# Cached pages compressed in runs of four and of two instead of one at a time, in a two-layer decoder trunk on one core

## The reference, cut to what matters

```
even layer:  xn = rms_norm(h);  q, k, v, z_a, u_b, v_b, z_b = xn @ w_in_ab     # 2048 x 9216
             dilated attention (A), spatial gating (B);  h += [A, B] @ w_out_ab
             h += sigmoid(h @ w_ple_gate[0]) * (p[0] @ w_ple[0])
odd layer:   the same frame around sparse attention (C), whose compressed branch reads
             pages = cache_c_cmp_kv[page_table]          # 8 rows x 16 pages of 128 x (K, V) x 4 heads x 128
             k_cmp, v_cmp = compress(pages, cw_k), compress(pages, cw_v)
compress:    block i = sum over 32 rows, i*16 .. i*16+31, of row * weight[row of the block, head]
```

## Time and profile before

| | |
|---|---|
| runs | 1836.01 us median, 1835.28 to 1836.19 |
| profiled execution | 1836.29 us, of which the span of instructions is 1834.6 us |
| mean granted clock | 0.989 |
| busy, share of the span | PE 96%, PEld 87%, DVE 59%, ACT 45%, POOL 10% |
| chain that ended last | PE 82%, DVE 12%, ACT 3%, issue 2%, DMA 1% |
| page matmuls (L1738) | 2432, one every 20 to 40 ns when they run |
| projection matmuls (L1712) | 9216 |
| DMA | 406 MB, mean 222 GB/s |

### The profile page before, as it was taken

How to read it: one execution, slowest core, us unless ns; L and a number is a source line. 1 busy time by engine, 2 the same in 40 slices (tenths; PEclk the granted TensorE clock), 3 DMA queues, 4 the chain that set the end, 5 groups by cost and what they waited for, 6 DMA issues and landing times.

```text
span 1834.6 us, 43768 instructions
## 1 busy us (share of the span) xinstructions
PE 1755.7 (96%) x17501; PEld 1597.3 (87%) x17501; DVE 1083.1 (59%) x1847; ACT 822.8 (45%) x1715; POOL 188.7 (10%) x360
## 2 busy tenths in 40 slices
PE   6999999988999989999989999999999999999999
PEld 5899999888888878988977997888988888889998
DVE  4478888767644445443565898664355444465454
ACT  4334434454334323334456554444355555444454
POOL 3000000000000000000000002333232434300000
PEclk9999999999999989999999999999999999999999
DMA  7987777643587738885655556888776888855454
GB/s 239 314 270 259 262 262 264 230 151 116 153 266 263 254 120 272 281 280 194 198 185 163 145 164 191 252 248 260 225 248 212 275 258 274 255 198 178 162 183 140
DMA packets 287096, 406.49 MB, mean 222 GB/s; under 512 B 18640, under 2 KB 223087, under 8 KB 285880
## 3 DMA queue, kind: packets, MB, share of 16 engines
q1 hardware_dynamic: 260196, 320.00, 54.1%
q0 software_dynamic: 26624, 83.92, 14.4%
q10 hardware_dynamic: 92, 0.02, 0.0%
HBM read 391.43 MB, written 12.45 MB: 220 GB/s over the span
## 4 chain that ended last, share of the span: by engine, by line
PE 82%; DVE 12%; ACT 3%; issue 2%; DMA 1%; SPq 0%; ACTq 0%; DVEq 0%
PE PJ L1712 53%; PE XB L1738 5%; PE XB L2117 4%; PE XB L2129 2%; DVE w_low L1066 2%; PE XB L2203 2%; PE XB L2184 2%; PE XB L2008 1%; DVE scr L1085 1%; PE XB L1851 1%; PE XB L2159 1%; PE XB L1754 1%; PE XB L1811 1%; PE XB L1890 1%; ACT w_up L652 1%
## 5 line engine op out<-in xcount | busy, mean ns | idle before, releaser
L1712 PE MATMUL PJ<-xh,w_up 128*128 128x264 f32 x3072 | 925.0, 301 | 30.0 <-DVE xl L1109 15.7
L1712 PE MATMUL PJ<-xl,w_up 128*128 128x264 f32 x3072 | 877.2, 286 | 0.0
L1712 PE MATMUL PJ<-xh,w_low 128*128 128x264 f32 x3072 | 875.9, 285 | 0.0
L1066 DVE TENSOR_TENSOR w_low<-wring,w_up 128x512 fp32r<-128x512 f32 x768 | 526.4, 691 | 445.8 <-ACT w_up L652 435.5
L652 ACT CAST w_up<-wring 128x512 fp32r<-128x512 f32 x768 | 473.9, 619 | 474.6 <-PE PJ L1712 467.9
L1712 PEld LDWEIGHTS PJ<-xh,w_up 128*128 128x128 f32 x3072 | 583.9, 190 | 64.6 <-issue 29.5
L1712 PEld LDWEIGHTS PJ<-xl,w_up 128*128 128x128 f32 x3072 | 583.8, 190 | 2.0
L1712 PEld LDWEIGHTS PJ<-xh,w_low 128*128 128x128 f32 x3072 | 581.4, 189 | 0.0
L620 POOL DMA_DIRECT2D cring<-in_cache_c_sel_kv_dram x256 | 137.8, 538 | 1371.9 <-issue 1076.1
L913 ACT COPY kcmp<-XB 128x512 f32<-128x512 f32 x80 | 46.9, 586 | 136.6 <-PE XB L2117 136.5
L1414 DVE COPY kcmp<-XB 128x512 f32<-128x512 f32 x80 | 55.3, 692 | 81.2 <-PE XB L2117 79.9
(11 more groups left out here) (326 smaller groups left out, 1501.2 us busy)
## 6 DMA issues: line engine op xcount, KB each, us to landing
wring<-in_w_in_ab_dram SPq DMA_DIRECT2D x144, 512.0 KB, 4.4
cring<-in_cache_c_cmp_kv_dram SPq DMA_DIRECT2D x128, 512.0 KB, 3.7
cring<-in_cache_c_sel_kv_dram POOLq DMA_DIRECT2D x256, 256.0 KB, 3.8
wring<-in_w_in_c_dram SPq DMA_DIRECT2D x112, 512.0 KB, 4.5
wring<-in_w_ple_gate_dram SPq DMA_DIRECT2D x64, 512.0 KB, 4.4
cring<-in_cache_a_kv_dram SPq DMA_DIRECT2D x48, 512.0 KB, 5.2
wring<-in_w_out_ab_dram SPq DMA_DIRECT2D x32, 512.0 KB, 5.3
cring<-in_cache_c_win_kv_dram POOLq DMA_DIRECT2D x64, 256.0 KB, 4.5
```

Of the source, the lines that this page charges most:

```text
L1066: nc.vector.tensor_tensor(w_low[:, e % NE], raw(e), w_up[:, e % NE].bitcast(F32), ALU.subtract).then_inc(sem("w_lo"), 1)
L1712: ins = nc.tensor.matmul(PJ[(2 * bl + c) % 4][:, 0:T], w[:, e % NE, k, tileT(c)], x[:, kx, :], start=(kx == 0 and w is w_up and x is xh), ...
```

## The change

`beside` calls `compress` four times in a row behind slot 7 of each block in rounds 1 to 4, ahead of the sums of squares. `beside_out` calls it twice in a row behind slots 3 and 7, in the output projection and in the first four blocks of the gating. SP asks for the four pages of a block in a row in rounds 1 to 4; to keep the order of the waits, it asks for quarter 0 of the next block ahead of them. In the output projection and gating SP's list stays as it was.

```diff
+            quarter(4, w_ab, 1, 0, 0)
             with sp.Fori(0, 4) as i:
                 for bl in range(4):
-                    for q in range(4):
+                    for q in range(1, 4):
                         quarter(i * 4 + (4 + bl), w_ab, i + 1, bl, q)
-                        page(i + 1, 0, bl, q)
+                    quarter(i * 4 + (5 + bl), w_ab, i + 1, bl + 1, 0)
+                    for n in range(NP):
+                        page(i + 1, 0, bl, n)
...
             for m in range(16):
                 for q in range(4):
-                    quarter(AB2 + m, w_ab, 5 + m // 4, m % 4, q)
+                    if m or q:
+                        quarter(AB2 + m, w_ab, 5 + m // 4, m % 4, q)
...
                 for bl in range(4):
                     def beside(s):
-                        if s % 2 == 1:
-                            compress(r, bl, s // 2, 1, 0)
+                        if s == SLOTS - 1:
+                            for n in range(NP):
+                                compress(r, bl, n, 1, 0)
...
             def beside_out(m, s):
 
-                if s % 2 == 1:
-                    compress(m // 4, m % 4, s // 2, 6, 32)
+                if s % 4 == 3:
+                    for n in range(s // 2 - 1, s // 2 + 1):
+                        compress(m // 4, m % 4, n, 6, 32)
```

## The result

The changed kernel takes 1816.55 us (median of 4 runs, 1814.21 to 1819.96) against 1836.03 before; the ratio is 0.9897, 95% interval 0.9881 to 0.9912. It is 1.0% faster. 1814.3 was forecast, with a range of 1808 to 1824. The profiled execution took 1816.02 us, its span 1814.3.

A forecast was written before the change was run, and what follows sets the result against it. TensorE was taken as the bound (busy 96% of the span, 82% of the chain). Visits saved, DVE's hold and `wple` summed to 27.4 - 4.0 - 1.7 = 21.7 us off, giving 1814.3 us by the median, range 1808 to 1824.

The forecast's parts named there:

- The price of a visit: TensorE, between projection matmuls: going over to page matmuls and back costs 0.38 us each visit.
- The term of 72 visits: TensorE: 48 fewer visits in rounds 1 to 4, 24 fewer in output projection and gating, saving 27.4 us.
- a joint between pages: TensorE, pages back to back: the boundary between two pages was taken to cost nothing; at worst 0.38 us.
- DVE holds slot 7: Rounds: DVE's split of e = 7 makes slot 7 late by 0.27 us in 15 blocks, 4.0 us.
- The DMAs of the rounds: Rounds 1 to 4: four page requests in a row delay quarter 1 without TensorE waiting; taken as nothing.
- wple: Block 43: load lands 0.9 us later and the block's own 0.76 are lost, 1.7 us; wait about 5.2.
- the time of the request: SP, block 43: page 0 released at about +7.2; quarter, second page and `wple` requested at about +8.4.
- The clock: After the wait for `wple`: a longer wait may move or lengthen the 0.50 stretch; none taken, 2 us kept for the range.
- (a): Rival: nothing bites, DVE is just in time and `wple` comes sooner with block 43; 1808.6 us, chance 0.16.
- (b): Rival: DVE bounds the rounds, splits e = 5 to 7 late by 0.6 us or more; 1820 to 1829, chance 0.12.
- (c): Rival: the price is per page, so pages in a row pay it too; 1842 us, slower, chance 0.06.
- (d): Rival: page bursts make weights late in the rounds, 2 us in 16 blocks; 1846 us, slower, chance 0.04.

The follow-up runs named there:

- e3: The kernel before, with every page of rounds 1 to 4 cut into K and V halves, 8 visits a block instead of 4: 1860.14 us, ratio 1.013.
- e7: The changed kernel with 128 columns of weights instead of 32 in all page matmuls (not the reference's compressed pages): 1992.26 us.
- e1: The changed kernel with the four `ones` matmuls of the last slot ahead of the run of four pages instead of behind it: 1812.38 us.
- e2: The changed kernel with wple asked for at the start of the output projection instead of behind the gating's second page: 1810.68 us.
- e4: The changed kernel with runs of two pages behind slots 3 and 7 in the rounds too, SP's list there as before: 1819.21 us.
- e6: The kernel before, with 128 columns of weights instead of 32 in all page matmuls (not the reference's compressed pages): 1991.43 us.
- e5: The changed kernel with `ones` ahead of pages, wple asked for early, and runs of four in output projection and gating, SP's list reordered there: 1800.61 us.

## Why the prediction was right

- *The price of a visit*, 0.38 us: 0.36 by e3, and in the output projection (15.33 - 14.62) / 2 = 0.355. The term of 72 visits was 27.4 and is 25.9. That a joint between pages costs nothing was taken from the 32-matmul page, and it held: 80 in a row keep its pace.
- *DVE holds slot 7*: right in place, mechanism and size. Forecast 4.0 us, or 0.27 a block; 4.4 by the waits, 0.27 a block by e7 alone, 0.28 by block 17 of e1. Missed were blocks 8 and 12, the first of a round behind the start of a new pass of the loop: DVE's chain runs 0.23 us later there, before and after alike. It had reserve before and has none now, so these two took 15.17 us instead of 14.93.
- *The DMAs of the rounds*: as forecast, nothing. The median from issue to landing of a page rose from 3.5 to 5.3 us in rounds 1 to 4, and TensorE waits for none there.
- *wple*: the mechanism was right, the size short. The wait became 6.26 us, not 5.2, and the net loss of block 43 is 1.84 us beside its own lost 0.72, against 0.9 and 0.76: the term of 1.7 is 2.6. The failed step is the time of the request, +8.4; it goes out at +10.04. The release was forecast right, +7.2: the first 32 of the 48 page matmuls end 1.11 us after 785.12, at +7.17. But the page's request goes out 0.76 us behind that, as it did before (805.76, when the page's matmuls end, to 806.52), and the next page's, whose buffer is free by then, 0.77 us behind the end of the quarter's (787.90 to 788.67). The sum had neither. SP reads the page's number from the table at these places; that this is what takes the time was not tried. From request to landing it was 10.9 us, 0.5 less than the 11.4 that I had, which made up for a third of the error by chance.
- *The clock*: I had left it at nothing, and nothing it was. It stood at 0.5 for 3.4 us more, but that was within the wait. In `ple` the low clock costs 1.4 us against e2 (15.94 and 14.51), and it cost 1.6 before (16.10). This was luck in part: in e4 the same wait left `ple` at 17.36, 2.9 over e2.
- *The rivals*: (a) falls with the 15 waits, (b) with their size, (c) with e3 and with the run of 80, (d) with the absence of any DMA among the waits of the rounds.

The sum was 27.4 - 4.0 - 1.7 = 21.7. With what was measured it is 25.9 - 4.4 - 2.6 = 18.9, which is what the changed stages gained. The profiled spans differ by 20.3 and the medians by 19.5, so the forecast looks better than its terms were, by the 1.4 us that the profiled executions differ in stages that nothing changed. Single executions of one kernel lie 6 to 8 us apart, so the last 2 us can't be told from chance.

## What to carry to other kernels

Matmuls on column groups of 32 between full-width ones cost 0.36 us for each visit here, whether 8, 16 or 80 of them ran in it: gather them into few runs. Full-width ones are no way out unless there are very few, since 16 take 1.79 us instead of 0.44; by these figures, an estimate, the two are even at about four. A run put at one place shortens all that lay between, so look at which engine's chain keeps its place (here DVE's, hung on the `ones` behind the run) and put whatever starts that chain ahead of the run. And a load that already ends late suffers first when the release ahead of it moves: its request belongs ahead of anything that waits on another engine.

## What the runs showed of the hardware that I had not expected

- The `ones` matmuls, of another type than the projection's but 128 wide, cost no passage. In e1, where they come first, they start 0.12 us behind the last projection matmul (296.57, 296.69), as the next one would; the pages start 0.21 behind it (302.58, 302.79). The four add some 0.9 us, an estimate: from 296.57 to the second projection matmul behind the run, at 300.26, it is 3.69 us, and a run of 80 with its passage is 0.24 + 2.20 + 0.36 = 2.80. That is 0.22 each, twice a full-width page matmul (0.11) for twice the columns. The page matmuls cost a passage only while they use column groups of 32 (e6 and e7, 20.64 and 20.62 us).
- The same wait of 6.3 us for `wple` left the clock at 0.5 for 6.8 us in one kernel and for 10.2 in another (e4); a wait of 3.56 us left it so for 3.4. Such stretches lie in different places in different executions: blocks 20 to 35, which no experiment changed, took 334.7 to 340.5 us in the profiled executions of e1 to e5, with the clock at 0.5 for different lengths near block 35. The length goes with the clock there: 334.7 us at a mean granted clock of 0.98 (e4), 338.9 at 0.97 (the changed kernel), 340.3 at 0.96 (e1). The whole executions of e4 go the same way: 1814.7 and 1816.7 us with a mean clock of 0.990 and 0.989, 1822.6 and 1823.0 with 0.985 and 0.986. So the clock has a large part in the spread; what sets it from one execution to the next was not shown.
